# A pair's score chunks issued together, and the transposes woven into the projection tiles

## The reference

```python
def _mla_branch(x, w_in, q_norm, w_q_up, kv_norm, w_kv_up, w_out):
    h = x @ w_in
    cq, ckv, k_rope, gate = h[..., :c1], h[..., c1:c2], h[..., c2:c3], h[..., c3:]
    q = (_rmsnorm(cq, q_norm) @ w_q_up).reshape(B, S, MLA_HEADS, MLA_NOPE_DIM + MLA_ROPE_DIM)
    kv = (_rmsnorm(ckv, kv_norm) @ w_kv_up).reshape(B, S, MLA_HEADS, MLA_NOPE_DIM + MLA_V_DIM)
    ...
    o = _dense_causal(q_full, k_full, v, scale).reshape(B, S, MLA_WIDTH)
    return (o * jax.nn.silu(gate)) @ w_out
```

## Time and profile before

| what | value |
|---|---|
| median of 3 runs | 1684.19 us |
| lowest and highest run | 1683.74 and 1685.02 us |
| span of the profiled execution | 1682.5 us |
| PE busy | 1651.9 us |
| DVE, ACT, POOL busy | 775.0, 767.3, 658.7 us |
| granted clock of TensorE, mean of the span | 1.000 |

### The profile page before, as it was taken

One profiled execution on the slowest core, in us unless ns is written; L12 is line 12 of the kernel. 1 busy time (PEld: TensorE's weight loads), 2 busy tenths in 40 slices (PEclk: granted clock), 3 DMA queues, 4 the chain that ended last, 5 costly groups with the idle time before them and its releaser, 6 DMA issues.

```text
span 1682.5 us, 24607 instructions
## 1 busy us (share of the span) xinstructions
PE 1651.9 (98%) x9349; PEld 1340.9 (80%) x9349; DVE 775.0 (46%) x2038; ACT 767.3 (46%) x1565; POOL 658.7 (39%) x551
## 2 busy tenths in 40 slices
PE   8999999999999999999999999999999999999998
PEld 8777779777888787788777778777788888888877
DVE  3767636566343434336767636888141111001052
ACT  4566724566243535524566635336753222222252
POOL 5333224332243424234332224792154444444423
PEclk9999999999999999999999999999999999999999
DMA  6323144323442322153223145432153333333322
GB/s 171 70 45 77 47 160 134 78 67 68 150 141 76 82 59 79 48 173 110 62 45 85 47 155 154 118 90 74 49 166 101 100 97 92 100 101 88 125 63 88
DMA packets 216048, 161.19 MB, mean 96 GB/s; under 512 B 53755, under 2 KB 197147, under 8 KB 215932
## 3 DMA queue, kind: packets, MB, share of 16 engines
q1 hardware_dynamic: 205904, 130.21, 27.6%
q10 hardware_dynamic: 9804, 29.38, 5.5%
q0 software_dynamic: 224, 0.03, 0.1%
HBM read 148.32 MB, written 11.14 MB: 95 GB/s over the span
## 4 chain that ended last, share of the span: by engine, by line
PE 66%; DVE 8%; ACT 4%; POOL 1%; issue 1%; ACTq 0%; DMA 0%; DVEq 0%; SPq 0%; POOLq 0%
PE banks L530 33%; PE banks L481 6%; PE banks L483 6%; PE banks L482 6%; PE banks L751 3%; PE banks L712 3%; PE banks L766 3%; PE banks L612 3%; ACT AB L1501 1%; DVE misc L2642 1%; ACT G L1630 1%; DVE banks L2344 1%; DVE banks L2333 1%; DVE AB L2346 1%; PE banks L735 1%
## 5 line engine op out<-in xcount | busy, mean ns | idle before, releaser
L2844 POOL TENSOR_TENSOR w_lo<-w_raw,w_hi 128x512 fp32r<-128x512 f32 (+2 forms) x506 | 618.1, 1248 | 995.1 <-ACT w_hi L1371 983.8
L1371 ACT ACTIVATE w_hi<-w_raw 128x1024 fp32r<-128x1024 f32 (+4 forms) x254 | 249.8, 995 | 158.9 <-PE banks L483 101.6
L530 PE MATMUL banks<-XTh,w_hi 128*128 128x512 f32 (+5 forms) x1216 | 279.6, 372 | 4.0 <-DVE XTl L2306 1.4
L530 PE MATMUL banks<-XTl,w_hi 128*128 128x512 f32 (+5 forms) x1216 | 270.9, 365 | 0.0
L530 PE MATMUL banks<-XTh,w_lo 128*128 128x512 f32 (+5 forms) x1216 | 270.7, 365 | 0.0
L530 PEld LDWEIGHTS banks<-XTh,w_hi 128*128 128x128 f32 (+2 forms) x1216 | 207.1, 187 | 48.8 <-issue 6.4
L530 PEld LDWEIGHTS banks<-XTl,w_hi 128*128 128x128 f32 (+2 forms) x1216 | 211.0, 187 | 37.9
L530 PEld LDWEIGHTS banks<-XTh,w_lo 128*128 128x128 f32 (+2 forms) x1216 | 211.0, 187 | 37.3
L481 PE MATMUL banks<-w_hi,OTh 128*128 128x512 f32 (+1 forms) x448 | 173.0, 386 | 0.6 <-DVE QKl L2069 0.5
L483 PE MATMUL banks<-w_hi,OTl 128*128 128x512 f32 (+1 forms) x448 | 167.9, 375 | 0.0
L482 PE MATMUL banks<-w_lo,OTh 128*128 128x512 f32 (+1 forms) x448 | 167.9, 375 | 0.0
(11 more groups left out here) (218 smaller groups left out, 2209.9 us busy)
## 6 DMA issues: line engine op xcount, KB each, us to landing
w_raw<-in_w_gate_up_dram SPq DMA_DIRECT2D x44, 512.0 KB, 3.8
w_raw<-in_fox_w_in_dram SPq DMA_DIRECT2D x30, 512.0 KB, 4.1
w_raw<-in_mla_w_in_dram SPq DMA_DIRECT2D x26, 512.0 KB, 4.9
w_raw<-in_w_in_dram SPq DMA_DIRECT2D x24, 512.0 KB, 3.8
w_raw<-in_w_down_dram SPq DMA_DIRECT2D x22, 512.0 KB, 3.5
w_raw<-in_swa_w_in_dram SPq DMA_DIRECT2D x20, 512.0 KB, 3.8
w_raw<-in_mla_w_out_dram SPq DMA_DIRECT2D x16, 512.0 KB, 3.7
x_spill<-AB ACTq DMA_DIRECT2D x16, 512.0 KB, 2.8
```

Source lines behind the costliest of these rows:

```text
L530: mm = nc.tensor.matmul(o, wt[:, k, :], xt[:, k, lo:hi], start=first and n == 0 and k == 0, stop=last and n == 2 and k == nk - 1, skip_gro ...
L1371: nc.scalar.activation(view(w_hi, u, RING), view(w_raw, u, RAW), ACT.Copy).then_inc(hi_done, 1)
L2844: ins = pool.tensor_tensor(low[at], raw[at], high[at].bitcast(F32), ALU.subtract)
```

## The change

PE: a causal pair's chunks become (1), (2, 0), (3), and each gets fixed banks: chunk (1) banks 4 and 5, which the transposes use as well, chunk (2, 0) banks 0 and 1, chunk (3) banks 2 and 3. All chunks of a pair are issued together, after the round's projections and ahead of `mix`; FOX's and REL's added terms follow behind all chunks. The first score chunk waits until ACT has copied every transpose of the round (`pt_free`); the first transpose of the next round waits until DVE has read chunk (1) (`ps_free`). The six bursts of transposes are laid ready in `woven` and run inside the round's projection tiles, between their products; `values`, `rope` and the halves of FOX's values get places for that too.

ACT: the copies of the transposes (`turned`) come first in a round; then, in MLA's odd rounds, rope and query; the second head's exponentials follow the first's. DVE: the maxima of all three chunks come together, behind all of the round's other work and ahead of `mixed`; `norm_last` is gone; in MLA's odd rounds the first half of the keys moves behind the first head's `norm`.

```diff
-                self.s_chunks = [(0, 1), (2, 3)] if self.window else [(2, 0), (1,), (3,)] if sel else [(2, 0), (3,), (1,)]
+                self.s_chunks = [(0, 1), (2, 3)] if self.window else [(1,), (2, 0), (3,)]
+                self.s_banks = (0, 2) if self.window else (4, 0, 2)
...
+                            if (n * KD + k) % 6 == 5:
+                                weave()
...
+                    for ch, chunk in enumerate(pr.s_chunks):
+                        if i:
+                            pe.wait_ge(ps_free, s_first[i - 1] + ch + 1)
+                        if pr.s_banks[ch] == 4 and i >= 2:
+                            pe.wait_ge(pt_free, t_first[i - 2] + 2 * len(pr.t_chunks))
+                        for t in chunk:
...
+                    if x == ch == 0 and i + 1 < n_pairs and 4 in pr.s_banks:
+                        pe.wait_ge(ps_free, s_first[i + 1] + 1)
...
+                    elif i < n_pairs - 1:
+                        if i == 0:
+                            fill(i, 0)
+                        woven.append(next_turn)
+                        if i:
+                            fill(i, 0)
+                        fill(i, 1)
+                        fill(i, 2)
+                        woven.pop()
+                        while todo:
+                            next_turn()
+                        scores(i + 2)
+                        mix(i)
+                        fill(i, 3)
...
+                        if k < 2:
+                            weave()
                     end(mm)
+                    weave()
...
-                        exps(i + 1, 1)
-                    fill(i, 0)
+                    if i <= 0:
+                        fill(i, 0)
                     turned(i)
+                    if i > 0:
+                        fill(i, 0)
+                        fill(i, 4)
                     gated_high(i - 1)
...
                     fill(i, 5)
-                    if i not in exps_first:
-                        exps(i + 1, 1)
+                    exps(i + 1, 1)
...
                     fill(i, 0)
-                    maxima(i + 2, 0)
-                    maxima(i + 2, 1)
+                    if i < 0:
+                        maxima(i + 2)
+                    fill(i, 4)
                     gated_low(i - 1)
-                    fill(i, 4)
                     norm(i + 1, 0)
                     if i in norm_first:
                         norm(i + 1, 1)
                     fill(i, 1)
-                    if i not in norm_last and i not in norm_first:
+                    if i not in norm_first:
                         norm(i + 1, 1)
                     fill(i, 2)
-                    maxima(i + 2, 2)
                     if i < 0:
                         fill(i, 3)
+                    else:
+                        maxima(i + 2)
                     mixed(i)
-                    if i in norm_last:
-                        norm(i + 1, 1)
                     fill(i, 6)
```

More of the change, by code:

```diff
@@ L689, in pair_attention, with scores @@
                 t_first = [c.tch + 2 * len(pairs[0].t_chunks) * i for i in range(n_pairs)]
-                def scores(i, ch):
-                    if not 0 <= i < n_pairs or ch >= len(pairs[i].s_chunks):
+                n_chunks = len(pairs[0].s_chunks)
+                s_first = [c.sch + n_chunks * i for i in range(n_pairs)]
+                def scores(i):
+                    if not 0 <= i < n_pairs:
                         return
                     pr = pairs[i]
-                    if ch == 0 and a0 + i in ready_q:
+                    if a0 + i in ready_q:
                         groups_stored(pe, ready_q[a0 + i])
-                    if ch == 0 and a0 + i in ready_rope:
+                    if a0 + i in ready_rope:
                         pe.wait_ge(rope_done, ready_rope[a0 + i])
[L699 to L702, removed]
                     def at(t):
@@ L705, in at @@
                                 slice(pr.s_col(t), pr.s_col(t) + pr.keys[t]))
[L707 to L715, removed]
+                    for ch, chunk in enumerate(pr.s_chunks):
[4 more added lines that the diff above has]
+                        for t in chunk:
+                            ts, ks, cols = at(t)
+                            for n, (qp, kp) in enumerate(((QKh, QKh), (QKh, QKl), (QKl, QKh))):
+                                for x in range(2):
+                                    r = slice(HD * x, HD * x + HD)
+                                    mm = nc.tensor.matmul(bank[pr.s_banks[ch] + x][:, cols], qp[r, pr.q, ts], kp[r, pr.k, ks],
+                                                          start=n == 0 and t == chunk[0],
+                                                          stop=n == 2 and pr.rope is None and not pr.aug and not (pr.sel and t),
+                                                          skip_group_check=True)
+                        if pr.rope is not None:
+                            for t in chunk:
+                                ts, ks, cols = at(t)
+                                for n, kp in enumerate((QKh, QKl)):
+                                    for x in range(2):
+                                        r = slice(HD * x, HD * x + HD)
+                                        mm = nc.tensor.matmul(bank[pr.s_banks[ch] + x][:, cols], pr.rope[r, ts], kp[r, 7, ks],
+                                                              start=False, stop=n == 1, skip_group_check=True)
+                        if not (pr.aug or pr.sel):
+                            mm.then_inc(ps_done, 1)
@@ L716, in scores @@
+                    if pr.aug and i % 2 == 0:
+                        pe.wait_ge(aug_in[pr.aug[2]], 16 * 4)
                     if pr.sel:
                         pe.wait_ge(ident_round, 1)
[L718 to L736, removed]
@@ L737, in scores @@
-                    mm.then_inc(ps_done, 1)
-                    c.sch += 1
+                    if pr.aug or pr.sel:
+                        for ch, chunk in enumerate(pr.s_chunks):
+                            if pr.sel:
+                                pe.wait_ge(sel_done, max(chunk))
+                            for t in chunk:
+                                ts, ks, cols = at(t)
+                                if pr.aug:
+                                    rows, r0, _ = pr.aug
+                                    for x in range(2):
+                                        r = slice(HD * x + r0, HD * x + r0 + 4)
+                                        mm = nc.tensor.matmul(bank[pr.s_banks[ch] + x][:, cols], rows[r, 6, ts], rows[r, 7, ks],
+                                                              start=False, stop=True, skip_group_check=True)
+                                elif t:
+                                    for x in range(2):
+                                        mm = nc.tensor.matmul(bank[pr.s_banks[ch] + x][:, cols], ident_r[:, :], SEL_R[t],
+                                                              start=False, stop=True, skip_group_check=True)
+                            mm.then_inc(ps_done, 1)
@@ L740, in turn @@
+                    c.sch += n_chunks
                 def turn(i, x, ch):
@@ L2203, in maxima @@
                     b = a % 2
-                    if ch == 0 and pr.window:
+                    if pr.window:
                         for x in range(2):
@@ L2209, in maxima @@
                         link(ins)
[L2210 to L2221 removed]
+                    for ch, chunk in enumerate(pr.s_chunks):
+                        dve.wait_ge(ps_done, c.sch + 1)
+                        for x in range(2):
+                            if ch == 0 and i >= 2:
+                                dve.wait_ge(pt_done, t_first[i - 2] + (x + 1) * len(pr.t_chunks))
+                            for t in chunk:
+                                o = bank[pr.s_banks[ch] + x][:, pr.s_col(t):pr.s_col(t) + pr.keys[t]]
+                                ins = nc.vector.tensor_tensor_reduce(pr.score(b, x, t), o, pr.bias(t, x), 1.0, -3e38,
+                                                                     ALU.add, ALU.max, mx[:, b, 4 * x + t:4 * x + t + 1])
+                        ins.then_inc(ps_free, 1)
+                        c.sch += 1
                     dve.wait_ge(ps_free, c.sch)
```

68 lines of the change are left out of this document (24 added, 44 removed).

## The result

The changed kernel takes 1718.23 us (median of 4 runs, 1715.64 to 1718.46) against 1684.54 us for the kernel before in the same comparison: 1.0198 times as long, 95% interval 1.0183 to 1.0212. The forecast was 1708 (1688 to 1721). The profiled execution, the shortest of the four, took 1715.64 us, with a span of 1713.8 against 1682.5, 31.3 more.

What follows compares the result with a forecast made beforehand. PE, busy 1651.9 of 1682.5 us, was taken as the bound. Net of saved visits, 19.5 + 3 - 1 - 1 + 2.5 = 23, first products +1: span 1706.5, median 1708 us, range 1688 to 1721 (own range 1697 to 1718).

Steps and rivals of the forecast that it cites:

- rival (c): FOX: if the key's bank also comes after the second norm, each round loses about 2 us more; 1720 us, chance 0.05.
- What PE saves: PE, all layers: fewer visits to the scores save 19.6 us: MLA 8.4, FOX 7.0, REL 1.8, SWA 2.4.
- MLA: +22.5 us: MLA, both layers: late projection banks cost +19.5 us in four double rounds (40.6 us, not 35.75), other rounds +3.
- FOX: -1 us forecast: FOX: gate tiles wait 0.5 to 0.8 us in five rounds, values after round 5 nearly 3; net -1 of -7.
- SWA: -1 us: SWA: tiles long enough except round 6's gate tile, which waits 2 to 3 us; net -1 us.
- REL: +2.5 us: REL: value tiles wait about 2.5 and 1 us for ACT's normalising, round 2's late copies about 2 more; +2.5 us.
- rival (d): PE's clock: falls to the lower level at the six longest waits, adding 8 us; 1716 us, chance 0.02.
- the term for first products: PE: the first product after a wait runs some 0.1 us longer, +1 us over a dozen waits of the chain.
- (b): Saving and waits cancel: MLA's chain 4.5 us shorter in two rounds; 1684 us, chance 0.04.
- (a): Only the saving shows, ACT and DVE free banks in time; MLA's chain about 6 us shorter; 1665 us, chance 0.12.
- the price of a visit: PE: each visit to the scores costs 0.3 us in MLA, 0.5 in FOX, because half-row products stand between full-row work.

Runs made afterwards that it cites:

- the last kernel: Against the kernel before: SWA and FOX with scores together, two bursts at the round's start, the rest woven; MLA and REL as before. 1674.13 us, ratio 0.9939, the fastest.
- the swap: Changed kernel with `mixed` put ahead of the next pair's maxima in MLA's rounds 1 and 3, nothing else changed; 1707.12 us, ratio 1.0128 to the kernel before.
- the version with two early bursts besides: Changed kernel with two bursts at the round's start, FOX argument removed, round 5's second norm behind the gate, `mixed` first in MLA's rounds 1 and 3; 1679.82 us.
- the kernel with the late `mixed`: Kernel before with DVE doing `mixed` six times over in MLA, so the value products' bank comes free later; 1713.79 us, ratio 1.0167.

## Why the prediction was right, and where it was short

The cause and its place were right, and the range held the result, but in part by luck. The forecast's own range, 1697 to 1718, ends 0.2 us below the measured median; the wider one reached to 1721 for a loss of 12 us in FOX, rival (c). What came on top was another thing: the clock, which had a chance of 0.02, and a smaller loss in FOX.

**What PE saves: 19.6 us, right.** PE's busy time fell by 11.2 us. The four stretches at 1.2 GHz add some 1.7 each to it, so at full clock it is 18.0; longer first products behind the added waits can account for the rest, which was not measured. The three score lines lost 11.2 us (127.9 to 116.7) where I had about 15. FOX and SWA alone, 9.4 by the prediction, give 1651.9 - 1644.0 = 7.9 in the last kernel, 9.6 without its one slow stretch.

**MLA: +22.5 us, right in its place and nearly in its size.** The double round came out at 41.1 us against 40.6 worked out. In the even round the last copy, `mixed` and the exponentials ended within 0.1 us of the schedule. The 0.5 us are ACT's in the odd round: the split between its exponentials, of 1024 columns, took 1.0 us (167.01 to 167.96) where I had 0.4. Five waits came at the predicted places: rope 0.40 (0.4), query 0.76 (1.1), second keys 1.74 (1.8), first values 0.95 (0.9), second values 2.51 (2.8). (The row of the rope product names POOL, but the query's low half ended at 154.41, 0.15 us ahead of it, and the query at 158.74 has the same distance from the `mixed` that frees its bank: the bank ended the wait.) Round 6's gate tile and first transpose waited 0.56 and 1.84. Both layers together lost 26.0; a slow stretch in the first accounts for 1.7 of the difference. That `mixed` behind the maxima sets the end is shown by the swap (11 us less), that the late copies set the rest by the version with two early bursts besides (another 3.2 us in a double round).

**FOX: -1 us forecast, +3.9 measured: the step that failed.** I took 0.5 to 0.8 for each gate tile. They waited 1.25, 0.84, 2.35, 1.76 and 0.85. The 2.35 comes from an argument that changes its meaning, which the diff shows and I did not follow into the call; it is worth 1.5 us. Rounds 0 and 3 were 1.4 us over my upper value together: there ACT has two splits ahead of the second head's exponentials, where I counted one for every round. ACT in rounds 1 and 3:

```profile
589.04 1.05 ACT L1391 ACTIVATE w_hi<-w_raw 128x1024 fp32r<-128x1024 f32 x1
...
652.71 2.00 ACT L1391 ACTIVATE w_hi<-w_raw 128x1024 fp32r<-128x1024 f32 x2
```

One slow stretch adds 1.7. -1 and these 4.6 make 3.6. That the query's bank ends these waits was right, though their rows name a weight split (L1391): DVE's low half of the query ends 0.15 us ahead of each of the five tiles, the same distance as that from the gate to the SWA tile at 421.53 which waits for it, while in four of the five the split ends a few ns after the tile has begun.

**SWA: -1 us, right** at +0.65 with its slow stretch of 1.7 in it; its rounds take 15.97 us against 16.36. The wait for round 6's gate tile was 3.17 where I had 2 to 3.

**REL: +2.5 us, mis-sized**: +0.8. The waits were as feared, 5.5 us in its rounds against 1.6 before, and its rounds are 2.5 us longer; but the stretch ahead of its first value products is 1.7 shorter, more than the visits saved there (0.6) explain. I did not follow that further.

**The clock: rival (d) had 0.02, and happened.** I followed the rows, and the rows of the kernel before have no wait above 1.4 us behind which the clock could have shown anything, except the one at the very start, where PE had not yet worked. They were no evidence for waits of 2.5 us. The Trainium skill, page "TensorE: Matmul & The Clock Gate", Part 1, has an idle engine go back from 2.4 to 1.2 GHz. This trace agrees at four waits, behind which the clock reads 0.50, and the kernel with the late `mixed` agrees at all six of its new ones. Behind the eleven other waits of 1.7 us and more the clock held in this trace. The cost of (d), 8 us for six waits, was nearly of the right size for each: four stretches cost some 5 us in the span, as the one in MLA's second layer shortened the wait behind it (1.4 in place of 2.5).

So of the 31.3 us some 5.1 are the clock's, and 26.2 stand against the 24 of the forecast: 3.1 more in FOX, 0.8 more in MLA (with the term for first products counted there), 1.7 less in REL. The median lies another 2.6 us over the profiled execution. The other runs of the changed kernel have no trace, but their mean clocks are 0.994, 0.994 and 0.995 against 0.995 in the profiled one, so one or two more stretches at 1.2 GHz may be in them (not shown).

**Two rivals were priced by sums that don't agree.** A chain 6 us shorter in each of four double rounds takes 24 us off 1708 and gives 1684, the price of (b), and not the 1665 of (a); the 4.5 us of (b) give 1690. For 1665 the waits of the other rounds and layers would have had to go as well.

Still open: what decides whether the clock falls behind a given wait, whether the price of a visit comes from the half-row products (no run takes them alone), and whether the chunk in the transposes' banks costs anything by itself. It is in FOX in every new version, the fastest included; it was not tried alone.

## What to carry to other kernels

Where the bounding engine's order changes, work out when each buffer that it needs next comes free: an engine at 45% is late when its instructions stand in the wrong order, and the mending is then a swap in its list. Work that seems badly placed may be the cover of another engine's chain: move it only as far as the chain stays hidden (with two bursts first, the rest woven and two norms moved, the idea that lost 2% gains 0.6% in SWA and FOX). When a diff removes a parameter, follow the positional arguments of every call.

## What the runs showed of the hardware

Behind waits of PE of 1 to 3.5 us (or at their end) TensorE was found at 1.2 GHz, mostly for 3.4 us, in two places for 6.8 and once for 17, and there a product of 512 columns took 0.43 us in place of 0.23 (with the late `mixed`, starts at 239.00 and 239.43 in a stretch, at 243.83, 244.05 and 244.28 after it). Behind the six new waits of 2.8 to 3.5 us it fell each time; behind waits of 2.50 and 0.98 it fell in some profiles and not in others, with the same instructions around them, and behind SWA's wait for round 6's gate tile it fell in the changed kernel (3.17) and held with MLA as before (3.16). So with the late `mixed` time lost to waits cost more than the waits. Runs of one kernel differ with the clock: 1676.5 to 1685.7 for one with such waits, at mean clocks of 0.998 and 0.993, against 1674.0 to 1675.9 for the fastest. The kernel before is not free of it: one of its runs took 1692.0 us at a mean clock of 0.994, the others beside it 1683.5 to 1685.7 at 0.998 to 1.000.
